# Gated-linear-attention heads: the two decay products take other accumulator banks, and 24 projection matmuls are issued ahead of the previous head's last transposes

## The reference, cut to what matters

```
log_a = log_sigmoid(a1 @ w_a2 + b_a2) / 16          # a1: (frames, 16), one head: 128 decay channels
b     = cumsum(log_a)                               # within a block of frames
q_t, k_t = q * exp(b), k * exp(-b)
s     = causal(q_t @ k_t.T)
o     = s @ v + q_t @ S
S     = exp(b_last) * S + (k * exp(b_last - b)).T @ v
out   = rmsnorm(o) * g_head * silu(z)               # then the output projection
```

## Time and profile before

| | before |
|---|---|
| median of 3 runs | 1701.48 us (1700.59 to 1703.48) |
| the profiled execution's own time | 1703.87 us |
| its span, first to last instruction | 1701.8 us |
| mean granted clock of TensorE | 0.96 of 2.4 GHz |
| busy: PE, DVE, ACT, POOL | 1589.4, 959.6, 629.6, 184.6 us |
| GLA heads, from the first decay product to the last transposes | 837.3 to 1061.1 us of the span |

### The profile page before, as it was taken

How to read it: one execution, slowest core, us unless ns; L and a number is a source line. 1 busy time by engine, 2 the same in 40 slices (tenths; PEclk the granted TensorE clock), 3 DMA queues, 4 the chain that set the end, 5 groups by cost and what they waited for, 6 DMA issues and landing times. The chain is left out here.

```text
span 1701.8 us, 31184 instructions
## 1 busy us (share of the span) xinstructions
PE 1589.4 (93%) x11168; PEld 1445.6 (85%) x11168; DVE 959.6 (56%) x2102; ACT 629.6 (37%) x1491; POOL 184.6 (11%) x384
## 2 busy tenths in 40 slices
PE   5999999997999999899699998899999999978898
PEld 2689898986999999799689888888888888866798
DVE  1665565554666656734565554476577667653632
ACT  2523232322222222423544442344545454443521
POOL 1000000000000000001000001023122212311000
PEclk9999999998999999899799999999999999997999
DMA  9433342423451433224333312311211111020223
GB/s 316 112 109 100 94 111 81 119 60 99 81 149 57 117 95 96 70 82 127 90 60 83 84 34 56 91 40 43 61 48 54 42 42 52 5 69 2 87 84 112
DMA packets 195259, 140.91 MB, mean 83 GB/s; under 512 B 18332, under 2 KB 178584, under 8 KB 194916
## 3 DMA queue, kind: packets, MB, share of 16 engines
q1 hardware_dynamic: 177772, 130.16, 27.2%
q10 hardware_dynamic: 17400, 9.60, 2.0%
HBM read 128.58 MB, written 11.15 MB: 82 GB/s over the span
## 5 line engine op out<-in xcount | busy, mean ns | idle before, releaser
L166 PE MATMUL bank<-hT,w_high 128*128 128x288 f32 x1152 | 368.6, 320 | 13.3 <-DVEq L1473 6.3
L167 PE MATMUL bank<-hT,w_low 128*128 128x288 f32 x1152 | 348.1, 302 | 0.0
L168 PE MATMUL bank<-hT,w_high 128*128 128x288 f32 x1152 | 347.4, 302 | 0.0
L166 PEld LDWEIGHTS bank<-hT,w_high 128*128 128x128 f32 x1152 | 225.1, 195 | 23.6 <-issue 8.4
L167 PEld LDWEIGHTS bank<-hT,w_low 128*128 128x128 f32 x1152 | 225.1, 195 | 0.0
L168 PEld LDWEIGHTS bank<-hT,w_high 128*128 128x128 f32 x1152 | 224.5, 195 | 0.0
L166 PE MATMUL bank<-output_w_split,gT_high 128*128 128x256 f32 x512 | 143.6, 280 | 0.0
L168 PE MATMUL bank<-output_w_split,gT_high 128*128 128x256 f32 x512 | 143.2, 280 | 0.0
L167 PE MATMUL bank<-output_w_split,gT_low 128*128 128x256 f32 x512 | 142.5, 278 | 0.0
L167 PEld LDWEIGHTS bank<-output_w_split,gT_low 128*128 128x128 f32 x512 | 96.7, 189 | 0.0
L166 PEld LDWEIGHTS bank<-output_w_split,gT_high 128*128 128x128 f32 x512 | 96.1, 188 | 0.1
(11 more groups left out here) (456 smaller groups left out, 3613.6 us busy)
## 6 DMA issues: line engine op xcount, KB each, us to landing
x<-in_w_in_even SPq DMA_DIRECT2D x72, 512.0 KB, 4.2
x<-in_w_in_odd SPq DMA_DIRECT2D x56, 512.0 KB, 4.2
x<-in_w_ada SPq DMA_DIRECT2D x32, 256.0 KB, 4.3
front_w_ada<-in_w_ada SPq DMA_DIRECT2D x6, 1024.0 KB, 13.6
output_w_raw<-in_w_out_even SPq DMA_DIRECT2D x12, 512.0 KB, 3.4
output_w_raw<-in_w_out_odd SPq DMA_DIRECT2D x12, 512.0 KB, 3.5
gdn_E<-G_rows SPq DMA_DIRECT2D x8, 576.0 KB, 5.0
gT<-in_w_ada SPq DMA_DIRECT2D x16, 256.0 KB, 4.2
```

The source lines that it names most:

```text
L166: pe.matmul(out, w[0], x[1], start=first, stop=False)
L167: pe.matmul(out, w[1], x[0], start=False, stop=False)
L168: return pe.matmul(out, w[0], x[0], start=False, stop=last)
```

## The change

- The decay products go to `wa_bank(n)`, PS[4] for n = 0 and PS[3] for n = 1, and ACT copies them from there. PE waits for the previous head's last reads of these banks (`kw_ready`, `v_copied`) before the first of them, and no longer for `qk_copied`.
- The first two query halves (ct = 0) no longer wait for the copies of the decay products; they wait only for the previous head's last copies.
- `turn_g(previous, T - 1)` moves from ahead of the query projection to behind its first half (24 passes).

In the heads of the other kinds nothing changes: for them NA is 0, so `n >= 2` and `ct` not zero say the same.

```diff
+        def wa_bank(n):
+            return PS[4 - n][:, 0:HALF]
...
                     if kind == "C":
                         pe.wait_ge(*wal.done(h, 15))
+                        pe.wait_ge(*kw_ready.before(h, 0))
+                        pe.wait_ge(*v_copied.before(h, 0))
                         for n in range(2):
-                            pe.wait_ge(*qk_copied.before(h, 0))
-                            pe.matmul(PS[n][:, 0:HALF], wa[:], M["a1T"][0:RANK, n * HALF:(n + 1) * HALF],
+                            pe.matmul(wa_bank(n), wa[:], M["a1T"][0:RANK, n * HALF:(n + 1) * HALF],
                                       start=True, stop=True).then_inc(qk_psum.sem, 1)
-                        if previous is not None:
-                            turn_g(previous, T - 1)
...
-                            pe.wait_ge(*(qk_copied.done(h, n - 2) if n >= 2 else qk_copied.before(h, 0)))
+                            pe.wait_ge(*(qk_copied.done(h, n - 2) if ct else qk_copied.before(h, 0)))
...
                             last.then_inc(qk_psum.sem, 1)
+                            if kind == "C" and n == NA and previous is not None:
+                                turn_g(previous, T - 1)
...
-                            act.activation(la[:, to], PS[half][:, 0:HALF], ACT.Identity, bias=M["vec"][:, bass.ds(h + 64, 1)]
+                            act.activation(la[:, to], wa_bank(n), ACT.Identity, bias=M["vec"][:, bass.ds(h + 64, 1)]
```

## The result

The changed kernel takes 1709.18 us (median of 14 runs, 1705.84 to 1720.78) against 1701.30 us for the kernel before beside it (14 runs, 1698.63 to 1705.24). The ratio is **1.0046, with a 95% interval of 1.0034 to 1.0058**: slower, by 5.8 to 9.9 us. Forecast were 1706.6 us and a range of 1703.5 to 1711.5 us, with 0.78 for slower. The execution of 1720.78 us stands apart, with a granted clock of 0.915 where the other thirteen have 0.960 to 0.965 and at most 1710.88 us. The profiled execution has 1709.60 us of its own and a span of 1707.6 us, 5.8 us more than before.

A forecast was written before the change was run, and what follows sets the result against it. PE, busy 93% of the span, was taken as the bound, waiting on DVE's and ACT's decay chain. Heads 0 to 3 gave 0 + 1.9 + 0.9 + 2.3 = +5.1 us: 1706.6 us, range 1703.5 to 1711.5.

The forecast's parts named there:

- What bounds: GLA heads: the 16.1 us decay chain on DVE and ACT has 0.5 to 0.7 us spare; PE pays further delay.
- The banks at nothing: Decay products' new banks: same work at other addresses, two added waits costed at nothing, a gain excluded.
- Head 1, +1.9 us: Head 1: later transposes delay the chain's end to 914.5 us, against the values' old start at 912.59: +1.9 us.
- the open term: Clock during head 1's passes: taken as full, though it fell to half at about 895.9 us before.
- Head 2, +0.9 us: Head 2: line 174 moves by 2.6 us, chain ends at 970.7 against 969.84 us: +0.9 us.
- Head 3, +2.3 us: Head 3: with 3.4 us of half clock, chain ends at 1026.9 against 1024.64 us: +2.3 us.
- the lower bound of 0.8: Head 3 with full clock throughout: chain ends at 1025.4 us, +0.8 us.
- Rival 1: Faster: PE's stream decides, chain has room; 1696.2 us, or about 1688.5 us if half clock went too; chance 0.05.
- Rival 2: No visible change: chain some 0.5 us shorter per head, clock full; +2.1 us, 1703.6 us; chance 0.17.
- Rival 3: Dearer: clock falls in PE's new stalls, one to three half-clock pieces of 1.6 us; 1708 to 1713 us; chance 0.23.
- The signs: Line 174 3 to 4 us later, heads 1 and 3; new PE waits of 2 to 5 us before n = 4.

The follow-up runs named there:

- the three places of the transposes: Changed kernel with the last tile's transposes behind 6, 24 (as changed) or 48 query passes: 1.0001, 1.0046 and 1.0079 of the kernel before.
- the banks alone: Changed kernel with the last tile's transposes put back ahead of the passes, new decay-product banks kept: 0.9985 of the kernel before.
- the run with block 2 early: Changed kernel with weight block 2 split before the exponentials instead of behind them, on ACT and DVE: 1.0054 of the kernel before.
- the two with the scaling later: Changed kernel, last tile's scaling moved behind the next head's shifts on DVE, transposes back ahead of the passes, run twice: 0.9978 and 0.9982 of before.
- the key banks: Changed kernel with the key halves' accumulators in banks of their own (n = 4 in PS[6], n = 5 in PS[5]): 1.0078 of before.
- the first run with the scaling later: Changed kernel with the last tile's scaling behind the next head's shifts on DVE, transposes still behind 24 passes: 0.9957 of before.
- the run with six passes: Changed kernel with the last tile's transposes behind 6 query passes instead of 24: 1.0001 of the kernel before.

## Why the prediction was right

- *What bounds.* The forecast said that DVE's chain has 0.5 to 0.7 us of room and that its delay is paid by PE. The profile after, the three places of the transposes and the scaling moved away show it.
- *The banks at nothing.* Right in its sign: the banks alone make the kernel no slower. I left out of the sum by parts that they gain in head 2 by themselves (1.6 us); together with the move this gain is hidden behind the later chain.
- *Head 1, +1.9 us*: 2.0 us measured. Transposes forecast 4.5 us behind the products and found at 4.56, line 174 forecast 5.2 us behind them (898.3 - 893.12) and found at 5.32, the chain 16.1 and 16.13, the two stalls 2.2 each and 1.92 and 1.94. Full clock in the passes, the open term, was right for this execution. It isn't a rule: in the run with block 2 early PE's stream up to the transposes is the same, and there they came 7.60 us behind the products.
- *Head 2, +0.9 us*: 2.6 us measured. The step that failed is the clock during the 24 passes: I took full clock, but it fell at the first pass and stayed at half for 3.4 us, so that the transposes came at +6.05 us instead of +4.5. The 1.6 us of that pass on to the values one to one.
- *Head 3, +2.3 us*: 0.9 us measured, the lower bound of 0.8. Here I took half clock for 3.4 us and it was full. The two misses are the same term, with opposite signs, and cancel: 5.5 against 5.1 us in sum. That the sum came so near is luck in this part.
- *The rest of +7.9 us.* The two profiled executions differ by 5.7 us in their own times and the medians by 7.9. The execution before lies 2.6 us above its median, the one after 0.4 us above. The forecast of +5.1 us is below the interval's lower end of 5.8. As the execution after lies near its median, what is missing sits mostly in the execution before, which was slower than its kernel usually is, and from which the forecast took all its rows. One piece can be seen: its values of head 3 came at 20.6 us, with 6.8 us of half clock, while in three profiled executions of other kernels with the transposes ahead (banks alone, and the two with the scaling later) they came at 19.5 to 19.6. Against those, head 3 would lose 1.9 us, not 0.9, and the sum would be an estimated 6.5 us. That the kernel before usually runs like them was not measured.
- *Rival 1*, PE's stream decides, is out: half clock at the boundaries did shrink by 10 us, and the time rose. By itself the rule in the Trainium skill, "TensorE: Matmul & The Clock Gate", section "Loop structure matters more than you think", was borne out in part: passes that follow at once had full clock at two of three boundaries, but half clock for 3.4 us in head 2. It says nothing of who waits.
- *Rival 2*, a shorter chain, is out: the chain took 16.13 or 16.14 us in each of heads 1 to 3.
- *Rival 3*, a clock that falls behind the new stalls, isn't out by the number, since 1709.18 us lies in its 1708 to 1713 us as well as in the range. The profiled execution speaks against it: the granted clock was 1.00 in the 3.6 to 4 us behind all three stalls ahead of the values. Half clock did follow the 4.15 us stall ahead of n = 4 in head 2, and the wait for the chain hid it.
- *The signs.* The waits came where they were forecast. One sign was wrong: line 174 was to come 3 to 4 us later behind the products than before in heads 1 and 3, and came 2.5 and 2.2 us later. The prediction's own sum has 5.2 - 2.8 = 2.4 us for head 1, so the slip is in the sign and not in the sum.

## What to carry to other kernels

Before an instruction is moved back on the busiest engine, look at what its result releases and what stands behind that wait in the stream of the engine that takes it: here half a microsecond of scaling held back a chain of 16 us. The remedy is to move the consumer as well, to a place where its engine waits anyway. That took the changed kernel from 0.5% slower than before to 0.4% faster, and some 0.2% of this is what the moved transposes gain by themselves. And a stall taken away ahead of a later one can merely make the later one longer; with the key banks this cost more than the two did apart.

## What the runs showed of the hardware that I had not expected

- The length of a stall alone doesn't tell whether TensorE's clock falls behind it. With banks for the key halves, single stalls of 4.08, 5.65 and 4.08 us ahead of the values had a granted clock of 0.58 to 0.60 behind them, over some 6 us. After the changed kernel's stalls of 1.92 us (at 903.14) and 1.94 us (at 914.48), with passes between them, the values were 0.12 us apart, which is full clock. But stalls of 2 us ahead of the values of head 2 went either way: 1.98 us with the banks alone kept full clock, 2.00 us in the first run with the scaling later and 1.99 us in the second with the transposes ahead did not. The stretches behind these three, in this order (PEclk, 1.00 or 0.67, is the seventh figure):

```profile
967.00:973.00 6.00, 5.14 (x38) 4.83 (x39) 2.26 (x7) 1.28 (x4) 0.00 (x0) 1.00 0.70 178
```

```profile
965.40:970.50 5.10, 4.95 (x27) 4.71 (x27) 0.62 (x2) 0.38 (x1) 0.00 (x0) 0.67 0.82 206
```

```profile
968.90:974.00 5.10, 4.95 (x27) 4.71 (x27) 0.68 (x2) 0.38 (x1) 0.00 (x0) 0.67 0.82 206
```

  What makes the difference was not found, and so it isn't shown either that one stall in two pieces keeps the clock.
- A busy PE in the profile is not a PE at full clock: in head 2 of the run with six passes it had no gap at all (7.00 of 7 us) and a granted clock of 0.53, the lower level, from the decay products on (1.93 us where head 1's in the changed kernel take 1.23). What set the clock back there was not tried.

```profile
948.00:955.00 7.00, 7.00 (x26) 5.65 (x26) 2.79 (x17) 1.15 (x3) 0.59 (x2) 0.53 0.06 21
```
